# Modulation vectors of a two-block network: 22 of 24 weight slabs multiplied on GpSimd instead of TensorE

## What is computed

```
h = conv(rmsnorm(x) @ w_up)        # 1024 -> 2 x 2816, depthwise over 3 tokens
x = x + (silu(gate) * val) @ w_down
```

```
shift, scale, gate       = split(silu(c)     @ w_mod + b_mod)   # for the tokens
shift_c, scale_c, gate_c = split(silu(c_ctx) @ w_mod + b_mod)   # for the context
h = rms_norm(x, norm_g) * (1 + scale) + shift
```

## Time and profile before

| | |
|---|---|
| three runs | 2966.12, 2966.87, 2967.13 us (median 2966.87) |
| profiled execution | span 2965.5 us (the page gives no time around it) |
| TensorE busy | 2901.6 us, 98% |
| VectorE busy | 1477.4 us, 50% |
| ScalarE busy | 1163.9 us, 39% |
| GpSimd busy | 146.0 us, 5% |
| DMA | 260.98 MB, 24 of them modulation slabs of 1 MB |

### The profile page before, as it was taken

The page is one execution under the profiler, slowest core; times in us unless marked ns, Lnnn a source line. Parts: engine busy times, 40 slices in busy tenths (PEclk is TensorE's granted clock), DMA queues, the critical chain, the costliest instruction groups (busy, mean ns, idle before and its releaser), DMA issues.

```text
span 2965.5 us, 38348 instructions
## 1 busy us (share of the span) xinstructions
PE 2901.6 (98%) x15438; PEld 2393.2 (81%) x15438; DVE 1477.4 (50%) x2051; ACT 1163.9 (39%) x1856; POOL 146.0 (5%) x199
## 2 busy tenths in 40 slices
PE   9999999999999999999999999999999999999998
PEld 7778888776788887877888788868888788888776
DVE  5655455546463657366252543263455735453454
ACT  5444333526452344146233431173232743341452
POOL 1000000110000000100000300100001000200100
PEclk9999999999999999999999999999999999999999
DMA  5343332331332222210112221311113022321322
GB/s 185 122 158 105 113 128 85 129 130 38 136 107 98 99 87 76 82 54 22 60 43 76 85 68 57 101 60 64 57 64 101 21 82 78 108 91 66 121 75 85
DMA packets 48844, 260.98 MB, mean 88 GB/s; under 512 B 6872, under 2 KB 7904, under 8 KB 24896
## 3 DMA queue, kind: packets, MB, share of 16 engines
q1 hardware_dynamic: 36288, 213.75, 20.8%
q0 software_dynamic: 12416, 45.25, 4.5%
HBM read 250.50 MB, written 4.28 MB: 86 GB/s over the span
## 4 chain that ended last, share of the span: by engine, by line
PE 91%; DVE 4%; ACT 3%; DMA 1%; issue 1%; POOL 0%; SPq 0%; DVEq 0%; ACTq 0%
PE PS L897 15%; PE PS L898 15%; PE PS L899 15%; PE PS L874 7%; PE PS L876 7%; PE PS L875 7%; PE PS L833 3%; PE PS L835 3%; PE PS L834 3%; PE PS L1124 2%; PE PS L1086 1%; PE PS L1197 1%; PE PS L1179 1%; PE PS L1166 1%; PE PS L944 1%
## 5 line engine op out<-in xcount | busy, mean ns | idle before, releaser
L897 PE MATMUL PS<-HHX,WHX 128*128 128x512 f32 (+1 forms) x1440 | 504.6, 350 | 0.4 <-DVE WLX L2409 0.3
L898 PE MATMUL PS<-HL,WHX 128*128 128x512 f32 (+1 forms) x1440 | 503.4, 350 | 0.0
L1680 ACT ACTIVATE WHX<-W 128x2048 fp32r<-128x2048 f32 (+1 forms) x102 | 174.8, 1713 | 560.9 <-DMA W<-in_w 379.2
L899 PE MATMUL PS<-HHX,WLX 128*128 128x512 f32 (+1 forms) x1008 | 350.1, 347 | 0.0
L2409 DVE TENSOR_TENSOR WLX<-W,WHX 128x2048 fp32r<-128x2048 f32 x60 | 137.5, 2292 | 344.9 <-ACT WHX L1680 344.8
L897 PEld LDWEIGHTS PS<-HHX,WHX 128*128 128x128 f32 x1440 | 272.7, 189 | 38.3 <-DVE WLX L2409 1.5
L898 PEld LDWEIGHTS PS<-HL,WHX 128*128 128x128 f32 x1440 | 272.7, 189 | 34.9
L874 PE MATMUL PS<-HH,WH 128*128 128x512 f32 x672 | 261.7, 389 | 0.0
L876 PE MATMUL PS<-HH,WL 128*128 128x512 f32 x672 | 261.7, 389 | 0.0
L875 PE MATMUL PS<-HL,WH 128*128 128x512 f32 x672 | 261.6, 389 | 0.0
L2409 DVE TENSOR_TENSOR WL<-W,WH 128x2048 fp32r<-128x2048 f32 x68 | 155.7, 2290 | 177.8 <-ACT WH L1680 177.7
(11 more groups left out here) (553 smaller groups left out, 5813.8 us busy)
## 6 DMA issues: line engine op xcount, KB each, us to landing
W<-in_w SPq DMA_DIRECT2D x172, 1024.0 KB, 4.8
XC<-in_wm POOLq DMA_DIRECT2D x12, 1024.0 KB, 5.2
H<-in_wm POOLq DMA_DIRECT2D x12, 1024.0 KB, 6.0
W<-in_wb SPq DMA_DIRECT2D x24, 512.0 KB, 3.3
W<-in_w SPq DMA_DIRECT2D x8, 768.0 KB, 4.1
ARENA<-ARENA POOLq DMA_DIRECT2D x32, 128.0 KB, 2.3
ARENA<-mrow SPq DMA_DIRECT2D x12, 256.0 KB, 3.9
PR<-in_nbias POOLq DMA_DIRECT2D x12, 256.0 KB, 3.0
```

The source lines that it names most:

```text
L897: pe.matmul(dst, wh[:, s, c], hi[:, k, t0:t1], start=k == 0, stop=False)
L898: pe.matmul(dst, wh[:, s, c], lo[:, k, t0:t1], start=False, stop=False)
L899: mm = pe.matmul(dst, wl[:, s, c], hi[:, k, t0:t1], start=False, stop=k == kb - 1)
L1680: act.activation(dst[:, s, 0:n], W[:, s, 0:n], ACT.Copy).then_inc(wh_ready[s], 1)
```

## The change

The slabs 0 and 15 are still multiplied on TensorE, in `pe_mod_first`, which stands at the head of the norms before the first and the second FFN, ahead of the sums of squares. Each has now 16 matmuls (the two columns of silu(c) separately, with 8 stationary columns each), accumulated in bank 4 into two halves of 256 columns. The other 22 are multiplied in `pool_mod` by GpSimd: 14 (slabs 1 to 14) from the moment when the first FFN's normed input is complete, 8 (16 to 23) from the same moment of the second FFN. Each is eight products of 128x512 (a k tile of the slab, repeated for the two vectors, times a column of silu(c) and one of silu(c_ctx), each repeated over 256) and seven additions into a place of its own in `MACC`, which lies in a free part of the arena. Slab i + 2 is fetched when slab i is done, by the same queue. `pe_mod_rows` then sums each place over the partitions with a one-hot column, one matmul of 512 columns a slab, in four column groups: for the first group between the two units of the last down part of the first FFN, for the second ahead of the second FFN's second down part. `act_mod_out`, `pe_mod_sum` (four matmuls) and `dve_mod_save` follow, once for each group. The context's load waits for GpSimd's last slab. All `mods=` are gone, and with them `pe_mod` in the units, the token stages and the norms.

```diff
-MODS_EVEN = 19
-MOD_COLS = 20
+MOD_GROUPS = (0, 15, MODS)
+MOD_ROWS = 8
...
-    MODP = MASKS[:, :, :].rearrange("p a b -> p (a b)")
+    MODP = PR[:, 0:4 * P]
...
-    SCW = sb("SCW", [P, (KT + 1) * MOD_COLS - 2])
-    SC = SCW[:, MOD_COLS - 2:].rearrange("p (a b) -> p a b", b=MOD_COLS)[:, :, 0:2]
+    SCZ = sb("SCZ", [P, KT, 2, MOD_ROWS])
+    SC = SCZ[:, :, :, 0]
+    ONEHOT = sb("ONEHOT", [P, 2 * MOD_ROWS - 1])
...
+    MACC = ARENA[:, split_at + 4 * KT * SLAB + KT * T:][:, 0:16 * 2 * SLAB].rearrange("p (a b) -> p a b", a=16)
...
+    def mod_steps(slabs):
+
+        return (2 * KT - 1) * (slabs - 1 - int(slabs > MOD_GROUPS[1]))
...
+    def pe_mod_first(pe, group):
+
+        i = MOD_GROUPS[group]
+        pe.wait_ge(sem("sc_ready"), 1)
+        wait(pe, sem("mod_out"), group)
+        pe.wait_ge(mod_loaded[i % 2], 16 * (i // 2 + 1))
+        for half in range(2):
+            for c in range(2):
                 for g in range(4):
                     k = 4 * half + g
...
+                    mm = pe.matmul(PS[32 * g:32 * g + MOD_ROWS, 4, c * SLAB:(c + 1) * SLAB], SCZ[:, k, c, :],
+                                   mod_slab(i)[:, k, :], start=half == 0 and c == 0, stop=False,
                                    skip_group_check=True)
...
+    def pool_mod(pool, own, i):
+
+        row = i - MOD_GROUPS[int(i >= MOD_GROUPS[1])] - 1
+        acc = MACC[:, row, :].rearrange("p (c n) -> p c n", c=2)
+        made = [RST[:, T:2 * T], MODP]
+        pool.wait_ge(mod_loaded[i % 2], 16 * (i // 2 + 1))
+
+        def product(k):
+
+            dst = made[k % 2].rearrange("p (c n) -> p c n", c=2) if k else acc
+            wait(pool, mod_step, own.n - (1 if k < 2 else 0))
+            own.mark(pool.tensor_tensor(dst, mod_slab(i)[:, k, :].unsqueeze(1).broadcast_to([P, 2, SLAB]),
+                                        SC[:, k, :].unsqueeze(2).broadcast_to([P, 2, SLAB]), ALU.mult))
+
+        def add(k):
+
+            pool.wait_ge(mod_step, own.n - (1 if k + 1 < KT else 0))
+            own.mark(pool.tensor_tensor(acc, acc, made[k % 2].rearrange("p (c n) -> p c n", c=2), ALU.add))
+
+        product(0)
+        product(1)
+        for k in range(1, KT):
+            if k + 1 < KT:
+                product(k + 1)
+            add(k)
+
+    def pe_mod_rows(pe, group):
+
+        first, end = MOD_GROUPS[group:group + 2]
+        pe.wait_ge(mod_step, mod_steps(end))
+        for row in range(end - first - 1):
+            g, o = row % 4, MOD_ROWS - 2 - row // 4
+            mm = pe.matmul(PS[32 * g:32 * g + MOD_ROWS, 4, :], ONEHOT[:, o:o + MOD_ROWS], MACC[:, row, :],
+                           start=False, stop=row + 5 >= end - first, skip_group_check=True)
+        mm.then_inc(sem("mod_rows"), 1)
...
         if st.src == "load":
             pe_idle(pe, 26)
+        if st.g in ("ffn_norm0", "ffn_norm1"):
+            pe_mod_first(pe, int(st.g == "ffn_norm1"))
...
-        pe_mod(pe, st, st.mods)
...
     def pe_down(pe, st):
-        if takes_ctx(st):
-            pe_mod_sum(pe, 1, 3)
-        pe_mod(pe, st, min(st.mods, 1))
+        group = mod_group(st)
+        if group == 1:
+            pe_mod_rows(pe, group)
...
         pe_split_unit(pe, st, 0, tile_of(HIDH), tile_of(HIDL), (hid_lo, ready), kb=st.n, slots=(1,))
+        if group == 1:
+            pe_mod_sum(pe, group)
+        elif group == 0:
+            pe_mod_rows(pe, group)
...
-        pe_mod(pe, st, max(st.mods - 1, 0), 1)
-        if st["mod"] + st.mods == MODS and st.mods:
-            pe_mod_sum(pe, 0, 2)
         pe_split_unit(pe, st, 1, tile_of(HIDH), tile_of(HIDL), (hid_lo, ready), kb=st.n)
+        if group == 0:
+            pe_mod_sum(pe, group)
...
-        act.wait_ge(mod_used, MODS)
+        act.wait_ge(mod_step, mod_steps(MODS))
...
+        pool.memset(SCZ[:, :, :, :], 0.0).then_inc(consts, 1)
+        pool.memset(ONEHOT[:, 0:MOD_ROWS - 1], 0.0).then_inc(consts, 1)
+        pool.memset(ONEHOT[:, MOD_ROWS - 1:MOD_ROWS], 1.0).then_inc(consts, 1)
+        pool.memset(ONEHOT[:, MOD_ROWS:2 * MOD_ROWS - 1], 0.0).then_inc(consts, 1)
...
+            if st.kind == "up" and st.step0 == 0:
+                pool.wait_ge(h_ready, st["hr"])
+                pool.wait_ge(sem("sc_ready"), 1)
+                pool.wait_ge(sem("mod_rows"), 2 * st.layer + 1)
+                for i in range(*MOD_GROUPS[st.layer:st.layer + 2]):
+                    if i not in MOD_GROUPS:
+                        pool_mod(pool, own, i)
+                        pool.wait_ge(mod_step, mod_steps(i + 1))
+                    if i + 2 < MODS:
+                        pool.dma_start(mod_slab(i), wm[i + 2, :, :, :]).then_inc(mod_loaded[i % 2], 16)
```

More of the change, by code:

```diff
@@ L152, in plan_stages @@
     norm("H", "load", "mix0_norm")
-    units(["xa", "ga"], at="H", era="even", split=True, first=True, mods=2)
+    units(["xa", "ga"], at="H", era="even", split=True, first=True)
     add("lru", {**full(0, 1, 2, 3, n=2), **free(0, 1, 2, 3, n=2)})
-    units(["cp", "vb", "bp"], at="H", era="even", split=True, mods=3)
-    units(["res", "res"], at="Y", era="even", split=True, final=True, mods=1)
-    norm("H", "res", "ffn_norm0", mods=2)
+    units(["cp", "vb", "bp"], at="H", era="even", split=True)
+    units(["res", "res"], at="Y", era="even", split=True, final=True)
+    norm("H", "res", "ffn_norm0")
     for f in range(2):
@@ L163, in plan_stages @@
             add("down", {"it": 2, "ws": 2, "w8": 4, **full(0, 2, n=2), **free(0, 1, 2, 3, n=2)}, layer=f,
-                n=2 * n, step0=sum(PARTS[:part]), split=True, apart=True, final=part == len(PARTS) - 1,
-                mods=((2, 2, 1), (2, 0, 0))[f][part])
+                n=2 * n, step0=sum(PARTS[:part]), split=True, apart=True, final=part == len(PARTS) - 1)
         if f == 0:
-            norm("H", "down", "mix1_norm", mods=2)
-            units(["u", "q", "k"], at="H", era="odd", split=True, first=True, mods=3)
-            tok(["g", "v"], era="odd", split=True, final=True, mods=1)
+            norm("H", "down", "mix1_norm")
+            units(["u", "q", "k"], at="H", era="odd", split=True, first=True)
+            tok(["g", "v"], era="odd", split=True, final=True)
             add("sgu", {**full(0, 1, 2, 3), **free(0, 1, 2, 3)})
@@ L172, in plan_stages @@
             add("fox", {**full(0, 2, n=8), **free(0, 2, n=8), **full(4, n=16), **free(4, n=16)}, jobs=jobs)
-            assert base["mod"] == MODS_EVEN
-            units(["res", "res"], at="Y", era="odd", split=True, first=True, final=True, mods=1)
-            norm("H", "res", "ffn_norm1", mods=2)
+            units(["res", "res"], at="Y", era="odd", split=True, first=True, final=True)
+            norm("H", "res", "ffn_norm1")
     norm("both", "down", "final_norm")
@@ L650, in mod_slab @@
         return XC[:, :, :] if i % 2 == 0 else H[:, :, T:TA]
-    def mod_rows(i):
-        group = int(i >= MODS_EVEN)
-        first = MODS_EVEN if group else 0
-        return group, (i - first) // 2, i - first < 2
-    def pe_mod(pe, st, n, done=0):
-        for i in range(st["mod"] + done, st["mod"] + done + n):
-            if i == 0:
-                pe.wait_ge(sem("sc_ready"), 1)
-                pe.wait_ge(sem("mod_zero"), 1)
-            pe.wait_ge(mod_loaded[i % 2], 16 * (i // 2 + 1))
-            _, j, opens = mod_rows(i)
-            for half in range(2):
+    def mod_steps(slabs):
+        return (2 * KT - 1) * (slabs - 1 - int(slabs > MOD_GROUPS[1]))
@@ new lines, in mod_group @@
+    def mod_group(st):
+        if st.kind == "down" and (st.layer, st.step0) == (0, PARTS[0] + PARTS[1]):
+            return 0
+        if st.kind == "down" and (st.layer, st.step0) == (1, PARTS[0]):
+            return 1
+        return None
+    def pe_mod_first(pe, group):
[5 more added lines that the diff above has]
+            for c in range(2):
@@ new lines, in pe_mod_rows, with pe_mod_sum @@
+    def pe_mod_rows(pe, group):
[5 more added lines that the diff above has]
+                           start=False, stop=row + 5 >= end - first, skip_group_check=True)
+        mm.then_inc(sem("mod_rows"), 1)
+    def pe_mod_sum(pe, group):
+        pe.wait_ge(sem("mod_out"), group + 1)
+        wait(pe, sem("mod_saved"), group)
+        for b in range(4):
+            mm = pe.matmul(PS[:, 5, 16 * b:16 * b + 16], MODP[:, b * P:(b + 1) * P],
+                           PC[:, PCOL["mod_sum"]:PCOL["mod_sum"] + 16], start=True, stop=True,
@@ L682, in pe_mod_sum, with act_mod_out @@
                            skip_group_check=True)
         mm.then_inc(sem("mod_summed"), 1)
[L685 to L689 removed]
+    def act_mod_out(act, group):
+        act.wait_ge(sem("mod_rows"), 2 * group + 2)
+        wait(act, sem("mod_summed"), group)
+        act.activation(MODP, PS[:, 4, :], ACT.Copy).then_inc(sem("mod_out"), 1)
@@ L1727, in act_down @@
     def act_down(act, own, st):
-        if st["mod"] + st.mods == MODS and st.mods:
-            act_mod_out(act, 0, 2, MODS - 1)
+        group = mod_group(st)
+        if group == 1:
```

(5 more changed lines are left out.)

87 lines of the change are left out of this document (24 added, 63 removed).

## The result

The changed kernel takes 2972.20 us (median of 20 runs, 2963.84 to 2975.76) against 2966.43 (20 runs, 2963.28 to 2968.25) for the kernel before on the same chip: ratio 1.0017 [1.0011, 1.0024]. It is slower, by some 5 us, not by the 39 that were forecast.

What follows compares the result with a forecast made beforehand. TensorE, busy for 98% of the span, was taken as the bound. Removed -15.5, added +10.1, clock +3.3 and +1.7, GpSimd wait +31, second layer +8.4: +39 on 2965.5 gives 3004.5, as median 3006; range 2970 to 3024.

Steps and rivals of the forecast that it cites:

- TensorE waits for GpSimd: the window grows by 31: First FFN layer: TensorE reaches the row-collecting point at 540, GpSimd ends at 571, so the window grows by 31 us.
- GpSimd's time in the first window: First FFN layer: 292 us of GpSimd's own work plus port waits make 376, from 195.2 to 571.
- the port: First FFN window: VectorE instructions with two SBUF inputs exclude GpSimd for 101 us, some 17 overlapping GpSimd's waits or issues.
- Done before 552: Sign against the forecast: GpSimd's last addition of the first group ending before 552 would prove it wrong.
- The deadline: Collecting point in the first layer's last down part: TensorE must wait there until GpSimd's first group is done.
- The starts: Start of both FFN layers: low tiles and split wait for GpSimd operations, 7 us each, plus 1.7 clock.
- Who waited goes next: Shared SBUF port: VectorE and GpSimd exclude each other, and the one that waited goes next; basis of 7 us per start.
- HIDL: Down parts: last low hidden tiles come late; TensorE loses 2.5 us in the second layer, hidden in the first.
- rival 1: GpSimd in time in the first layer, under 1.1 us per operation; window +12.2, total +18.5, 2985 us; chance 0.16.
- The clock: Three norms that lost their slab pair: longer gaps bring 1.2 GHz stretches, 1.1 us each, 3.3 together.
- Removed and added matmuls: TensorE: modulation slabs and small sums removed, -15.5 us; opening slabs, rows, sums and memsets added, +10.1 us.
- rival 2: Port costs TensorE nothing: VectorE keeps it between low tiles, GpSimd is fast enough; -9, 2958 us; chance 0.13.

Runs made afterwards that it cites:

- e12: Changed kernel with both operands of each GpSimd product read as 512 plain columns, without repetition (modulation wrong): 2973.04 us, one run.
- e5: Changed kernel with 16 slabs in the first group and 8 in the second: 2985.91 us, ratio 1.0062 to the kernel before.
- e10: Changed kernel, FFN opening slabs behind the sums of squares, idle matmuls in three norms, HIDL ahead of WL split in each up part's last unit: 2958.60 us, ratio 0.9970.
- e14: e10 with the first group's one-hot rows moved between the two slabs of the first layer's last down unit: 2952.84 us, ratio 0.9957 to the kernel before.
- e8: Changed kernel with a one-column VectorE instruction behind each HL tile of the two FFN norms: 2993.26 us, ratio 1.0091 to the kernel before.
- e3: Changed kernel with fourteen of the fifteen GpSimd operations of each slab left out (modulation wrong): 2959.98 us, ratio 0.9980 to the kernel before.
- e1: Changed kernel with twelve idle matmuls behind the last sum of squares in the three norms that lost slabs: 2968.74 us, ratio 1.0009 to the kernel before.
- e7: Changed kernel run again without edit, for a second trace: 2972.53 us, ratio 1.0018 to the kernel before.

## Why the prediction was wrong, step by step

By the forecast's own bound of 0.2% the result is "same" (+0.17%), which had a chance of 0.04; the time is at the low end of the range (2970 to 3024), 34 us under the value forecast. It is slower, but not by the mechanism that was named. The step that failed is "TensorE waits for GpSimd: the window grows by 31".

- **GpSimd's time in the first window: forecast 376, measured 341** (191.45 to 532.68). Products at 1.00 instead of 1.23: 112 x 0.23 = 26 less. Waits for completion at 0.08 instead of 0.2: 98 x 0.12 = 12 less. Additions at 1.29 instead of 1.23: 6 more. That makes 260 of the 292, and leaves 81 for the port, where 101 - 17 = 84 was taken; added up directly, by how much the operations of the window last longer than the shortest of their kind, it is 79: this term held. Over a slab's 15 operations the mean is 1.14 us, where 1.23 was taken; the prediction's other estimate, 1.12, was the near one. The start was 3.7 us earlier. The forecast had the broadcast product bounded by 0.47 and 1.70 and took the addition's row for it; e12 shows that it wasn't the broadcast but the addition's row that misled. "Done before 552" had been named as what would prove it wrong.
- **The deadline itself is real.** e5 has it at 7.3 us, e10 at 3.1, and e14 takes it away. In the changed kernel there were 8 us of room, some of them only because HIDL had already made TensorE late.
- **The starts: forecast 7 + 1.7 each, measured 0.** "Who waited goes next" came from rows in which GpSimd issued back to back. VectorE's run of nine subtractions kept the port, at all 13 moves from one to the next. In the up units the rule held, at 49 of 49, so it was not wrong as such but at this place; what is different there no run tells. The Trainium skill's rule (SBUF — State Buffer, Who interferes with whom: who issues first has the pair for the whole instruction, the other blocks) agrees with the 7.05 us in that only one runs at a time, but by issue order alone the product of 191.45 would have gone ahead of the HL tile of 191.70, and it did not; at the 49 the GpSimd operation had started first, and went first. e8 shows how little was between the forecast and the truth: with one small instruction in the run each start costs 10.
- **HIDL: forecast 2.5 for the second layer, and hidden under the wait in the first.** Measured 9.2 more over six down parts, 7.8 of it in the first layer, where nothing covered it. This term, which rival 1 had at 9.5, is with the clock the largest of the losses: e3 takes 12.2 off with it, e10 some 9 by an order in which it isn't late.
- **The clock: forecast 3.3 for the norms.** Filling their gaps gives 2.4 to 3.5 (e1), not all of it by the clock. In all the clock is more, 0.9949 against 0.9981, up to 9.5 by the stretches and 7.8 by the runs' own slope (e7); stretches also stand behind HIDL waits (527.83 in the first profile, 418 and 531 in e1's). The profile shown had three stretches and is 8.4 us below the median; e7's had six and is 7.0 longer, of which three stretches are 5.1 at most.
- **Removed and added matmuls.** A slab alone is worth 1.14 (the unit with one, 40.80 to 63.78, is 22.98 long, 96 matmuls of 0.2275 are 21.84), not 1.20. The one ahead of the LRU is worth 0, not 1.8: a wait of 0.89 took its place (62.87), and the six slabs up to the first norm gave 5.7 = 5 x 1.14. The opening slab ahead of a norm costs 1.10, forecast 1.3; rows 3.54 + 1.83 = 5.4, forecast 5.8. This part held.

As measured: removed 17 x 1.14 and 1.2 for the sums, -20.6 (the attention's wait for the saved values, to go by the forecast, went from 0.7 to 1.2); added 2.2 (opening slabs) + 5.4 (rows) + 1.3 (sums) + 0.2 (memsets) + 0.5 (that wait) = +9.6; HIDL +9.2; clock up to +9.5: +7.7 at most, measured +5 to +6. The clock's share is a bound, so the account closes to about 2 us; with the 7.8 of the slope it is +6.0. Without the clock it is -1.8: the change would be level or a little faster. Rival 1 had the right state of GpSimd but paid for the starts; rival 2 had the right starts but nothing for HIDL. The truth is rival 1 without its starts, and the forecast had not put the two together.

## What to carry to other kernels

Work moved to GpSimd is not free for TensorE, even where GpSimd ends in time: look for the shortest slack in VectorE's queue of instructions with two SBUF inputs, here four in a row around the start of a down part, with 2.7 us to spare at the second, and take the tile that TensorE needs first out of that queue's end (e10, some 9 us). A gap that idle work used to fill has to be filled again when the work goes (e1, 2.4 to 3.5 us), and a wait that is hidden by another one comes out when that is mended (e10 to e14, 4 to 6 us). A price for a new operation should come from a row of the same operation; the nearest size is not enough.

## What the hardware did that was not expected

- Who gets the port is not one rule. Nine VectorE subtractions back to back kept it for 6.0 us against a waiting GpSimd product (7.05 us long, 1.05 of it work); with a one-column instruction between them the product took 1.06. In the up units of the same trace a waiting GpSimd operation went ahead of the next VectorE subtraction at 49 of 49 places, with nothing in between. What decides it was not found.
- A VectorE instruction with two SBUF inputs that starts while GpSimd issues a DMA can wait for that and for two products behind it: 2.3 to 2.7 us, three times in the changed kernel's trace, and 2.7 on the critical HIDL tile in e1. The HL tiles that start during such an issue (191.10, 796.44) were not held up.
- On GpSimd a 128x512 float32 product follows the last after 1.00 us, an addition in place after 1.29; a wait on its own last instruction adds 0.08.
- With gaps of 2.98 us in the same three places, one execution has one stretch at half clock behind them, another three: the same kernel spreads over 12 us (20 runs) and 6.8 (11 runs), and with idle matmuls in the gaps over 2.5 (11 runs).
